# The attention phase of a hybrid decoder step in a new order, and the recurrence's key products on GpSimd

## What is computed

```python
# A: per group, residue of the dilation and block of 128 queries; keys: own block and the one before
s = jnp.where(mask, jnp.einsum('bnqhd,bnkhd->bnhqk', qb, kk), -jnp.inf)
m = jnp.max(s, axis=-1, keepdims=True)
p = jnp.exp(s - m)
den = jnp.sum(p, axis=-1, keepdims=True)
o = jnp.einsum('bnhqk,bnkhd->bnqhd', p / den, vv)
# B: per chunk of 64 tokens
qe = q_ * jnp.exp(b_)
ke = k_ * jnp.exp(-b_)
att = jnp.where(causal, jnp.einsum('bhtk,bhsk->bhts', qe, ke), 0.0)
o = jnp.einsum('bhts,bhsv->bhtv', att, v_) + jnp.einsum('bhtk,bhkv->bhtv', qe, state)
kd = k_ * jnp.exp(b_last - b_)
new_state = jnp.exp(b_last) * state + jnp.einsum('bhsk,bhsv->bhkv', kd, v_)
```

## Time and profile before

| | |
|---|---|
| median of 3 runs | 2405.88 us (2405.0 to 2408.24) |
| the profiled execution | 2397.48 us, span 2395.7 us |
| mean granted clock of TensorE | 0.983 |
| busy in the span: TensorE matmul / weight load | 2278.5 us (95%) / 1838.7 us (77%) |
| VectorE / ScalarE / GpSimd | 1708.5 us (71%) / 807.3 us (34%) / 276.5 us (12%) |

### The profile page before, as it was taken

How to read it: one execution, slowest core, us unless ns; L and a number is a source line. 1 busy time by engine, 2 the same in 40 slices (tenths; PEclk the granted TensorE clock), 3 DMA queues, 4 the chain that set the end, 5 groups by cost and what they waited for, 6 DMA issues and landing times. The chain is left out here.

```text
span 2395.7 us, 36175 instructions
## 1 busy us (share of the span) xinstructions
PE 2278.5 (95%) x12996; PEld 1838.7 (77%) x12996; DVE 1708.5 (71%) x3345; ACT 807.3 (34%) x1705; POOL 276.5 (12%) x455
## 2 busy tenths in 40 slices
PE   7999999989999999999999998889899898999998
PEld 5788878767788888888878886667778636888887
DVE  5756668757775688888778886878888757556663
ACT  5332221112224431121122234776766524122121
POOL 1100012212210012222221220001010000000000
PEclk8999999989999999999999999999999999999999
DMA  8999999999995667778787797656454397434431
GB/s 260 247 279 322 285 277 274 265 263 280 281 298 186 194 215 237 263 253 271 242 255 244 249 330 264 217 199 210 145 207 154 123 311 303 180 119 163 170 136 68
DMA packets 271184, 553.40 MB, mean 231 GB/s; under 512 B 33392, under 2 KB 60480, under 8 KB 268896
## 3 DMA queue, kind: packets, MB, share of 16 engines
q1 hardware_dynamic: 200688, 358.77, 44.0%
q0 software_dynamic: 58000, 166.36, 26.2%
q10 hardware_dynamic: 12320, 25.96, 2.8%
HBM read 442.60 MB, written 191.50 MB: 265 GB/s over the span
## 5 line engine op out<-in xcount | busy, mean ns | idle before, releaser
L1653 PE MATMUL b_acc<-b_whi,a_hi 128*128 128x512 f32 x1792 | 706.5, 394 | 11.2 <-DVE b_wlo L1307 6.4
L1654 PE MATMUL b_acc<-b_wlo,a_hi 128*128 128x512 f32 x1792 | 700.7, 391 | 0.0
L1655 PE MATMUL b_acc<-b_whi,a_lo 128*128 128x512 f32 x1792 | 700.3, 391 | 0.0
L1057 ACT CAST b_whi<-b_w 128x2048 fp32r<-128x2048 f32 (+1 forms) x127 | 228.8, 1802 | 519.8 <-PE b_acc L1655 372.9
L1653 PEld LDWEIGHTS b_acc<-b_whi,a_hi 128*128 128x128 f32 x1792 | 338.5, 189 | 84.8 <-issue 8.4
L1655 PEld LDWEIGHTS b_acc<-b_whi,a_lo 128*128 128x128 f32 x1792 | 338.4, 189 | 71.2
L1654 PEld LDWEIGHTS b_acc<-b_wlo,a_hi 128*128 128x128 f32 x1792 | 338.7, 189 | 68.6
L1307 DVE TENSOR_TENSOR b_wlo<-b_w,b_whi 128x2048 fp32r<-128x2048 f32 (+1 forms) x127 | 273.0, 2151 | 84.4 <-ACT b_whi L1057 84.4
L1101 ACT ACTIVATE c_sm<-c_sm,c_ends 128x256 f32<-128x256 f32 (+1 forms) x384 | 172.4, 453 | 14.8 <-DVE c_ends L1455 14.7
L1455 DVE CUSTOM_DVE_ANT_0 c_sm<-c_p_s,c_mask 128x256 f32<-128x256 f32 (+1 forms) x384 | 117.4, 360 | 40.4 <-PE c_p_s L1742 39.3
L982 POOL DMA_DIRECT2D a_x<-tm x188 | 107.8, 581 | 249.6 <-DVE sT L1421 172.8
(11 more groups left out here) (374 smaller groups left out, 3478.4 us busy)
## 6 DMA issues: line engine op xcount, KB each, us to landing
b_w<-t SPq DMA_DIRECT2D x64, 1024.0 KB, 7.9
t<-in_w_in POOLq DMA_DIRECT2D x48, 1024.0 KB, 10.9
b_w<-in_w_in SPq DMA_DIRECT2D x47, 1024.0 KB, 8.3
a_x<-tm POOLq DMA_DIRECT2D x167, 256.0 KB, 7.0
tm<-b_st SPq DMA_DIRECT2D x128, 256.0 KB, 7.4
b_ck<-in_cache_kv_w POOLq DMA_DIRECT2D x96, 256.0 KB, 4.8
c_qk<-tm SPq DMA_DIRECT2D x96, 256.0 KB, 3.6
t<-t POOLq DMA_DIRECT2D x16, 1024.0 KB, 12.2
```

What stands on the lines that cost most here:

```text
L1057: nc.scalar.copy(whi[:, b % HI_RING, part, 0:w], w_raw[:, k, part, 0:w]).then_inc(w_hi, 1)
L1653: nc.tensor.matmul(out, stat_hi, mov_hi, start=first, stop=False)
L1654: nc.tensor.matmul(out, stat_hi, mov_lo, start=False, stop=False)
L1655: return nc.tensor.matmul(out, stat_lo, mov_hi, start=False, stop=last)
```

## The change

- The four kinds of transposes get a table each, and a place of their own in a step: outputs behind the scores, the recurrence's keys behind the sums, then P, then k or q. Outputs move from `q + 9` to `q + 8`, the keys from `t_at + 3` to `t_at + 2`; so every step that turns something is an even one.
- VectorE's and ScalarE's copies follow that order. VectorE masks the first unit, moves the outputs, masks the second unit, then copies P, then q or k. ScalarE copies the keys between the outputs and P.
- The two key products of a tile move from VectorE to GpSimd (`scale_keys`, semaphore `keyed_g`), a tile ahead of the square of an output; at the last tile of a block, behind that square. VectorE keeps the product of q. The keys' transposes wait for `keyed_g`, the product `within` and SyncE's loads for both semaphores.

```diff
-    turn_qk_at = {}
-    for i in range(N_TASK):
-        turn_qk_at[units[4 * i].q - 8] = (i, 1)
-        turn_qk_at[units[4 * i].q - 6] = (i, 0)
-        turn_qk_at[units[4 * i].q + 9] = (i, 2)
-    for n, at in t_at.items():
-        turn_qk_at[at + 3] = (n, 3)
+    turn_k_at = {units[4 * i].q - 8: i for i in range(N_TASK)}
+    turn_q_at = {units[4 * i].q - 6: i for i in range(N_TASK)}
+    turn_o_at = {units[4 * i].q + 8: i for i in range(N_TASK)}
+    turn_kd_at = {at + 2: n for n, at in t_at.items()}
+    turn_at = sorted((q, place, (i, a)) for a, place, of in ((1, 5, turn_k_at), (0, 5, turn_q_at), (2, 1, turn_o_at),
+                                                          (3, 3, turn_kd_at)) for q, i in of.items())
...
@@ SyncE, load_tile
                     if n >= 2:
                         sp.wait_ge(scaled_g, n - 1)
+                        sp.wait_ge(keyed_g, n - 1)
@@ GpSimd
+                def scale_keys(n):
+                    _, e, b = ge
+                    t = tile_cols(n)
+                    pool.wait_ge(gate_step, G_STEPS * (n // GBLK) + G_STEPS)
+                    pool.wait_ge(gqk_in[n % 2], 32 * (n // 2) + 32)
+                    nc.gpsimd.tensor_tensor(e[:, :, t], gqk[:, n % 2, 1, :, :], e[:, :, t], ALU.mult)
+                    nc.gpsimd.tensor_tensor(b[:, :, t], gqk[:, n % 2, 1, :, :], b[:, :, t], ALU.mult).then_inc(keyed_g, 1)
+
+                scale_keys(0)
                 for n in range(NT):
+                    if (n + 1) % GBLK:
+                        scale_keys(n + 1)
                     pool.wait_ge(go_evacd, n + 1)
...
                     nc.gpsimd.tensor_tensor(gjunk[:, :, :], y, y, ALU.mult).then_inc(go_mult, 1)
+                    if (n + 1) % GBLK == 0 and n + 1 < NT:
+                        scale_keys(n + 1)
@@ ScalarE, attend and recur
-                    if q - 3 in tile_of:
-                        kd_evac(tile_of[q - 3])
...
                         o_evac(sum_at[q][1].i)
+                    if q in turn_kd_at:
+                        kd_evac(turn_kd_at[q])
                     if q in turn_p_at:
                         pT_evac(turn_p_at[q][0])
@@ VectorE, scale_tile
                     V.scalar_tensor_tensor(out=z[:, :, t], in0=gqk[:, n % 2, 0, :, :], scalar=GK ** -0.5, in1=z[:, :, t],
-                                           op0=ALU.mult, op1=ALU.mult)
-                    V.tensor_tensor(b[:, :, t], gqk[:, n % 2, 1, :, :], b[:, :, t], ALU.mult)
-                    V.tensor_tensor(e[:, :, t], gqk[:, n % 2, 1, :, :], e[:, :, t], ALU.mult).then_inc(scaled_g, 1)
+                                           op0=ALU.mult, op1=ALU.mult).then_inc(scaled_g, 1)
@@ VectorE, attend
-                    for x in score_at.get(q, ()):
+                    for x in score_at.get(q, ())[0:1]:
                         mask_and_max(x)
-                    if q in turn_qk_at:
...
+                    if q in turn_o_at:
+                        o_move(turn_o_at[q])
+                    for x in score_at.get(q, ())[1:2]:
+                        mask_and_max(x)
                     if q in turn_p_at:
                         pT_evac(turn_p_at[q][1])
+                    if q in turn_q_at:
+                        q_evac(turn_q_at[q])
+                    if q in turn_k_at:
+                        k_evac(turn_k_at[q])
@@ TensorE, transposes and within
-                        pe.wait_ge(scaled_g, i + 1)
+                        pe.wait_ge(keyed_g, i + 1)
...
                     pe.wait_ge(scaled_g, n + 1)
+                    pe.wait_ge(keyed_g, n + 1)
@@ TensorE, attend
                     for x in score_at.get(q, ()):
                         scores(x)
+                    if q in turn_o_at:
+                        transposes(turn_o_at[q], 2)
                     for x in sum_at.get(q, ()):
                         sums(x)
-                    if q in turn_qk_at:
-                        transposes(*turn_qk_at[q])
+                    if q in turn_kd_at:
+                        transposes(turn_kd_at[q], 3)
                     for x in turn_p_at.get(q, ()):
                         transpose_p(x)
+                    if q in turn_k_at:
+                        transposes(turn_k_at[q], 1)
+                    if q in turn_q_at:
+                        transposes(turn_q_at[q], 0)
                     recur(q)
```

More of the change, by code:

```diff
@@ L446, in project @@
     LAST_Q = max(units[-1].q + 12, LATE + 11)
-    turn_qk_at = {}
-    for i in range(N_TASK):
-        turn_qk_at[units[4 * i].q - 8] = (i, 1)
-        turn_qk_at[units[4 * i].q - 6] = (i, 0)
-        turn_qk_at[units[4 * i].q + 9] = (i, 2)
-    for n, at in t_at.items():
-        turn_qk_at[at + 3] = (n, 3)
-    assert len(turn_qk_at) == 3 * N_TASK + NT
-    tqk_no = {turn_qk_at[at]: n + 1 for n, at in enumerate(sorted(turn_qk_at))}
+    turn_k_at = {units[4 * i].q - 8: i for i in range(N_TASK)}
[4 more added lines that the diff above has]
+                                                          (3, 3, turn_kd_at)) for q, i in of.items())
+    tqk_no = {what: n + 1 for n, (_, _, what) in enumerate(turn_at)}
     turned_first = {what: [sum(1 for i, a in tqk_no if a == kind and tqk_no[i, a] < n) for kind in range(4)]
                     for what, n in tqk_no.items()}
-    tqk_free = {what: (at + 1) // 2 for at, what in turn_qk_at.items()}
+    tqk_free = {what: (q + 1) // 2 for q, _, what in turn_at}
     def turn_with(chunk, half):
@@ L547, in project @@
         gqk_in, gv_in = [sem("d_gqk_in0"), sem("d_gqk_in1")], [sem("d_gv_in0"), sem("d_gv_in1")]
-        gate_step, scaled_g = sem("d_gate_step"), sem("d_scaled")
+        gate_step, scaled_g, keyed_g = sem("d_gate_step"), sem("d_scaled"), sem("d_keyed")
         kd_evacd, att_done, att_masked = sem("d_kd_evacd"), sem("d_att_done"), sem("d_att_masked")
@@ L1189, in attend @@
                         exps(x)
[L1190 to L1193, removed]
+                    if q in turn_o_at:
+                        ends_copy(turn_o_at[q])
+                    if q - 2 in turn_o_at:
+                        o_store(turn_o_at[q - 2])
                     recur(q)
@@ L1504, in scale_tile @@
                 def scale_tile(n):
-                    z, e, b = ge
+                    z = ge[0]
                     t = tile_cols(n)
```

## The result

The changed kernel takes **2389.22 us** in the median of 7 runs (2381.88 to 2397.61); the kernel before, measured beside it, 2405.0 (2396.58 to 2414.77). The ratio is 0.9937, with a 95% interval of 0.9914 to 0.9959: 15 us faster, between 10 and 21 by that interval. Forecast were 2390 us, a range of 2381 to 2403, and a fall of 16. The profiled execution of the changed kernel took 2381.88 us (span 2380.1).

The account below looks back on a forecast made before the run. The order in which busy TensorE and VectorE release each other was taken to bound attention's tile stretches. 29 - 5.6 - 4 - 3 = 16 us off the 2405.88 us median gave 2390 us, range 2381 to 2403.

Parts of the forecast that it names:

- The sum (16): Attention phase: 29 us of removable waits less 5.6, 4 and 3 us of costs, a net gain of 16 us.
- The waits that go (29): TensorE idle before transposes sharing bank c_p_qk: keys 14.0, outputs 13.0, q and k 2 us, all to go.
- Changes of shape (5.6): Outputs' loads between scores and sums: one more shape change per task, 33 in tile stretches at 0.17, costing 5.6 us.
- The new wait of q (4): q, turned behind the keys, waits for ScalarE to copy them out: 16 tiles at 0.25 us, 4 us lost.
- VectorE late (3): Tile stretches: VectorE late by its longer recurrence steps takes back 3 us of waiting, between 0 and 8.
- nothing booked for its relief: VectorE loses two products a tile, 10.6 us in all, said to be off the path and counted as no gain.
- Wrong if the keys' transposes wait: Sign against the forecast: the recurrence's keys' transposes on TensorE waiting for GpSimd's products.
- GpSimd's product (0.52): One key product of 256 columns on GpSimd, estimated at some 0.52 us, two per tile, no cost on the path.
- The gate stretches: First rival: the three gate stretches between tile stretches gain 6 to 7 us more, giving 2383 us; chance 0.09.
- the second rival: GpSimd's products hold VectorE up in the tile stretches, taking back 12 us, 2402 us, no change; chance 0.11.
- The waits didn't come back: Third rival claimed TensorE's 29 us reappear before scores and q while 7.8 us of shape changes stay, 2414 us; chance 0.10.

Follow-up runs that it names:

- the one repeat: The unchanged kernel before, profiled once more: attention took 421.5 us after 422.5, the four tile stretches 285.2 us after 285.4.

## Why the prediction was right, and where its steps were not

The time (2389.2 for 2390), the place of the gain and the readings named ahead came: keys' idle 2.7 for 3, outputs' 0.12 a group for 0.17, late tile 18.35 for 18.4, early tile 13.84 (1559.78 - 1545.94) for 14, the second-last pair of scores of the chain in the earlier trace rows 13.8 us earlier in spite of the 3.7 later start, and a stage behind it as long as before.

- **The sum (16).** In the four tile stretches, from scores to scores, the idle time ahead of TensorE's weight loads fell from 63.0 to 46.8 us, which is all but 0.2 of the 16.4. Of it, the 0.12 or 0.17 ahead of loads that differ in shape from the one before grew from 34.6 to 40.1, and the rest, the waits, fell from 28.4 to 6.7. The prediction had 5.6 more of shape, 29 of waits and 7 of them coming back.
- **The waits that go (29).** In size right: keys 14.0 to 2.7, outputs of the tile stretches 12.7 to 3.9, and what is left are changes of shape. What failed is the step "For the outputs it is the recurrence's products and the scores; the 13.0 of the tile stretches go", as if each place earned its own wait. The outputs' move alone cost 8.0 us there; what counts is the cover behind the outputs as well as ahead of them. In the change that cover is sums and P; with sums alone the tile stretches lose 11.8, with P alone 8.3. The sum came out because all moves were made at once.
- **Changes of shape (5.6).** Measured 5.5: 0.12 ahead of the outputs and 0.17 behind them, where one gap of 0.12 (scores to sums, without a row in the view) was.
- **The new wait of q (4).** Five waits of 0.56, one of 0.73 and ten of 0.12 to 0.19: 4.9. None of it is shape, since q stands behind P, which has its own. Right in place and cause, and nearly in size.
- **VectorE late (3), and nothing booked for its relief.** What came back beside the wait of q is 1.7: in eight early or middle steps k waits 0.17 to 0.26, and its load starts 0.17 to 0.18 us after VectorE's copy of the outputs, not after its longer recurrence steps. With q's that is 6.6, and 0.1 before the scores, where 7 were booked. Nothing for the relief was too little: without it the keys wait 7.0, and 3.7 us of the tile stretches are lost. The prediction let the relief "pay for the rest" and did not see that the keys' 14.0 hang on it in part. "Wrong if the keys' transposes wait" was thought of for GpSimd only; VectorE's third product was the one that could be late.
- **GpSimd's product (0.52).** 0.73; halving the columns of a 1.04 square didn't halve it. Harmless, since it waits 22.3 us for loads in the whole phase and nobody waits for it.
- **The rivals.** The gate stretches gained 0.3, not 6. GpSimd does hold VectorE up, as the second rival said, but one instruction of a tile at most: 0.1 us in all after the change. The waits didn't come back before the scores; in the runs where they came back they did so before q and k.

## What to carry to other kernels

Where several groups take turns in one buffer, write down for each what stands ahead of it and what behind it, and compare both with the time its copier needs, the copier's other work included; moving one group can push the wait on to the next, and only the whole set of places tells. Before work is moved to another engine because a result is late, look whether the producer makes that result last: here the sequence of three instructions gave 3.0 of 3.7 us. And read a change of half a per cent by the stage that it touches: in the one repeat each tile stretch came out within 0.2 us, where the time scattered by 16.

## What the runs showed of the hardware

VectorE and GpSimd can stand in each other's way, but narrowly. VectorE's product of two operands in SBUF took 0.42 us in every run where GpSimd was elsewhere, and 0.68 to 0.81 in three of 16 with GpSimd's products beside it in the old order:

```profile
1622.62 0.74 POOL L1013 TENSOR_TENSOR d_ge<-d_gqk,d_ge 128x256 f32<-128x256 f32 x1
1623.31 0.73 POOL L1014 TENSOR_TENSOR d_ge<-d_gqk,d_ge 128x256 f32<-128x256 f32 x1
1623.54 0.80 DVE L1523 SCALAR_TENSOR_TENSOR d_ge<-d_gqk,d_ge 128x256 f32<-128x256 f32 x1
```

The order of the starts decides which of the two is longer. Where GpSimd's product was already at work, VectorE's ended 0.28 to 0.29 us after it, if not later by its own 0.42; that is 13 products in the six runs with key products on GpSimd, of 0.43 to 0.98. Where VectorE's started first, it kept 0.42, and GpSimd's took up to 1.00 instead of 0.73:

```profile
1828.07 0.41 DVE L1523 SCALAR_TENSOR_TENSOR d_ge<-d_gqk,d_ge 128x256 f32<-128x256 f32 x1
1828.08 1.00 POOL L1013 TENSOR_TENSOR d_ge<-d_gqk,d_ge 128x256 f32<-128x256 f32 x1 [0.93 <-DMA d_gqk<-fm]
```

VectorE's masks and copies, with an operand in PSUM, kept 0.42 and 0.69 beside GpSimd. The Trainium skill (GPSIMD Engine Reference, Key points) says that the two share SBUF interfaces and contend where a VectorE instruction has two inputs in SBUF; these rows agree, with up to 0.56 us for one product.

A GpSimd product of 256 columns took 0.73 us with two buffers and 0.61 in place on one, against 1.04 for 512 columns. And a change of TensorE's shape cost 0.12 us ahead of sums or outputs that follow scores, and 0.17 ahead of P or keys that follow sums.
